# Four by-token tiles at once: 512 moving weight columns in place of 256

## What is computed

```python
def first_block(x, mem, ...):
    for layer in range(2):
        u = rms_norm(x, attn_norm_w[layer]) @ w_in[layer]       # 1024 -> 2560
        # layer 0: q, k, v, gate of 6 retention heads; layer 1: q, k, v of 6 differential heads
        # both: queries of 4 memory heads
        ...
        x = x + concat([o_main, o_mem]) @ w_out[layer]
        gu = rms_norm(x, ffn_norm_w[layer]) @ w_gate_up[layer]
        x = x + (silu(gate) * up) @ w_down[layer]

def second_block(x, ...):
    proj = rms_norm(x, norm_mix_w) @ w_in                       # 1024 -> 5648
    z, xbc, dt_raw, q, k, v, f_raw = split(proj)
    y_ssd = ssd_mixer(xbc, z, dt_raw, ...)                      # 16 heads, 2 groups, group RMS norm
    y_fox = fox_mixer(q, k, v, f_raw, ...)                      # 16 heads of 64: q and k normed per head,
                                                                # causal softmax with a forget bias
    x = x + concat([y_ssd, y_fox]) @ w_out
    x = x + conv_gated_mlp(rms_norm(x), ...)
```

## Time and profile before

| | before |
|---|---|
| device time, median of 3 runs | 1043.74 us (1040.57 to 1046.72) |
| device time of the profiled execution | 1040.6 us |
| its span, first to last instruction | 1038.8 us |
| granted TensorE clock, mean | 1.000 |
| PE busy | 1023.2 us, 98% of the span |
| DVE busy | 796.6 us, 77% |
| ACT busy | 635.1 us, 61% |
| HBM read | 172.39 MB, 167 GB/s over the span |

### The profile page before, as it was taken

One profiled execution on the slowest core, in us unless ns is written; L12 is line 12 of the kernel. 1 busy time (PEld: TensorE's weight loads), 2 busy tenths in 40 slices (PEclk: granted clock), 3 DMA queues, 4 the chain that ended last, 5 costly groups with the idle time before them and its releaser, 6 DMA issues.

```text
span 1038.8 us, 21815 instructions
## 1 busy us (share of the span) xinstructions
PE 1023.2 (98%) x7372; PEld 940.7 (91%) x7372; DVE 796.6 (77%) x1301; ACT 635.1 (61%) x1188; POOL 236.0 (23%) x204
## 2 busy tenths in 40 slices
PE   8999999999999999999999999999999999999998
PEld 7999988888889898888888899999898999999988
DVE  6875897877665988988777559978868579999843
ACT  7754776666555667766656456766666666656532
POOL 3200044544110000244543110000201024444300
DMA  8643476666655332666666664543343456555663
GB/s 299 183 134 100 124 223 193 186 195 180 200 187 184 122 103 71 211 192 186 191 188 188 195 196 144 178 153 117 121 123 123 141 163 184 183 183 182 189 197 98
DMA packets 52483, 174.36 MB, mean 168 GB/s; under 512 B 5952, under 2 KB 7232, under 8 KB 52288
## 3 DMA queue, kind: packets, MB, share of 16 engines
q1 hardware_dynamic: 52416, 173.46, 53.9%
HBM read 172.39 MB, written 1.05 MB: 167 GB/s over the span
## 4 chain that ended last, share of the span: by engine, by line
PE 56%; DVE 4%; ACT 2%; issue 1%; DMA 0%; DVEq 0%; SPq 0%; ACTq 0%
PE bank L769 9%; PE scores L765 8%; PE bank L765 7%; PE scores L769 6%; PE bank L767 6%; PE bank L768 6%; PE scores L767 3%; PE scores L768 2%; PE bank L795 2%; PE bank L796 2%; PE bank L797 2%; DVE ring_parts L1731 1%; ACT tmp L1519 1%; DMA ring_raw<-w_up 0%; PE bank L1151 0%
## 5 line engine op out<-in xcount | busy, mean ns | idle before, releaser
L1731 DVE TENSOR_TENSOR ring_parts<-ring_raw,ring_parts 128x1024 fp32r<-128x1024 f32 (+2 forms) x343 | 421.4, 1232 | 34.8 <-ACT ring_parts L1221 29.3
L1221 ACT ACTIVATE ring_parts<-ring_raw 128x1024 fp32r<-128x1024 f32 (+2 forms) x343 | 341.2, 997 | 64.2 <-PE scores L769 28.9
L769 PE MATMUL bank<-xw_parts,ring_parts 128*128 128x256 f32 x824 | 230.9, 280 | 0.0
L769 PEld LDWEIGHTS bank<-xw_parts,ring_parts 128*128 128x128 f32 x824 | 156.4, 190 | 0.0
L769 PE MATMUL scores<-xw_parts,ring_parts 128*128 128x256 f32 x528 | 147.3, 279 | 0.0
L767 PE MATMUL bank<-xw_parts,ring_parts 128*128 128x256 f32 x472 | 136.5, 289 | 0.3 <-DVE con L1876 0.2
L769 PE MATMUL bank<-act_parts,ring_parts 128*128 128x256 f32 x480 | 134.8, 281 | 0.0
L768 PE MATMUL bank<-xw_parts,ring_parts 128*128 128x256 f32 x472 | 133.4, 283 | 0.0
L765 PE MATMUL scores<-xw_parts,ring_parts 128*128 128x512 f32 x352 | 123.8, 395 | 0.7 <-DVE xw_parts L1737 0.7
L765 PE MATMUL bank<-xw_parts,ring_parts 128*128 128x512 f32 x352 | 123.4, 394 | 0.7 <-DVE xw_parts L1737 0.7
L795 PE MATMUL bank<-ring_parts,xw_parts 128*128 128x256 f32 x384 | 112.9, 294 | 0.2 <-DVE u L1919 0.2
(11 more groups left out here) (257 smaller groups left out, 2136.5 us busy)
## 6 DMA issues: line engine op xcount, KB each, us to landing
ring_raw<-w_up SPq DMA_DIRECT2D x132, 512.0 KB, 4.3
ring_raw<-w_in SPq DMA_DIRECT2D x85, 512.0 KB, 3.6
ring_raw<-w_down SPq DMA_DIRECT2D x48, 512.0 KB, 3.8
ring_raw<-w_down SPq DMA_DIRECT2D x24, 384.0 KB, 4.1
ring_raw<-w_oa SPq DMA_DIRECT2D x16, 256.0 KB, 2.6
ring_raw<-w_ob SPq DMA_DIRECT2D x16, 256.0 KB, 2.9
ring_raw<-w_oa SPq DMA_DIRECT2D x8, 512.0 KB, 3.6
ring_raw<-w_ob SPq DMA_DIRECT2D x8, 512.0 KB, 3.6
```

Of the source, the lines that this page charges most:

```text
L769: return mm(ps[:, 0:T], w_lo, high(parts, t), start=False, stop=stop)
L1221: A(ring_hi[:, slot * DM:slot * DM + width], ring_raw[:, slot * DM:slot * DM + width], ACT.Copy).then_inc(hi_done, 1)
L1731: V.tensor_tensor(ring_lo[:, a:b], ring_raw[:, a:b], ring_hi[:, a:b].bitcast(f32), SUB).then_inc(lo_done, 1)
```

## The change

What the diff does, part by part:

- Nine groups of four tiles each (`FOURS`: one in in0, two in in1, six in in2) take the place of eighteen pairs. A four holds the weights of 512 channels; each of its tiles has a quarter of the input rows (two blocks of 128) and 512 columns. `project_four` uses both banks at once, the first 128 tokens in one and the other 128 in the other: per tile six matmuls of 512 columns, then the steps that belong in the middle of the tile, then six more. A four is 48 matmuls of 512 columns where two pairs were 96 of 256; the count of TensorE rows falls from 4960 to 4528.
- A new semaphore, `first_tokens`, is raised in the last tile when the first bank is complete; DVE takes out each bank with one TENSOR_SCALAR of 128x512 (`evac_four`, L1870 of the new kernel): two instructions for two pairs as before.
- The tile orders change (`ORDER`): in in2 two query pairs stand together, then two key pairs, then four value tiles. Norms move with them: in layer 1 the ones of tiles 0 and 2 two slots later, in layer 2 the query and the key norm of a j are in neighbouring slots (24 and 25, 28 and 29, 36 and 37, 40 and 41) where they were two slots apart, and the values of the fox heads are read from slot 33 or 45 on.
- `after_like` puts `spread` and `norm_out` behind steps of the same kind where there are some. The per-head means have four buffers where there were two. `squares` of a norm whose norm n-2 is a per-head one waits for that one's head sum and not for its output.
- The host lays the weight columns out to match.

The diff, without the semaphore, the buffer's size and part of the host layout:

```diff
@@ -52,10 +52,11 @@
 SMALL = 44
-ORDER = {"in0": [18, 19, 0, 3, 6, 7, 1, 4, 8, 9, 2, 5, 10, 11, 12, 13, 14, 15, 16, 17],
+ORDER = {"in0": [18, 19, 0, 3, 1, 4, 6, 7, 8, 9, 2, 5, 10, 11, 12, 13, 14, 15, 16, 17],
          "in1": [18, 19, 0, 1, 6, 7, 2, 3, 8, 9, 12, 13, 4, 5, 10, 11, 14, 15, 16, 17],
          "in2": list(range(8, 20)) + [SMALL] + list(range(8))
-         + [t for j in range(4) for t in (20 + 2 * j, 21 + 2 * j, 28 + 2 * j, 29 + 2 * j, 36 + 2 * j, 37 + 2 * j)]}
+         + [t for j in range(0, 4, 2) for t in (20 + 2 * j, 21 + 2 * j, 28 + 2 * j, 29 + 2 * j, 22 + 2 * j, 23 + 2 * j,
+                                                30 + 2 * j, 31 + 2 * j, *range(36 + 2 * j, 40 + 2 * j))]}
@@ -116,6 +117,9 @@
+FOURS = {"in0": (6,), "in1": (0, 2), "in2": (20, 22, 24, 26, 36, 40)}
...
 HALVES = ("up0", "up1", "down0", "down1", "down2")
@@ -127,6 +131,10 @@
             self.wide = [c for c, t in enumerate(ORDER.get(name, [])) if t in BY_TOKEN[name] and t % 2 == 0]
+        self.fours = [ORDER[name].index(t) for t in FOURS.get(name, ())]
+        for c in self.fours:
+            self.wide.remove(c + 2)
+            self.wide.append(c + 1)
         self.name, self.n, self.blocks, self.ring0, self.out0 = name, n, blocks, ring0, out0
@@ -148,7 +156,11 @@
-        return c in self.wide or c - 1 in self.wide
+        return c in self.wide or c - 1 in self.wide or self.of_four(c) is not None
+    def of_four(self, c):
+        return next((c - a for a in self.fours if a <= c < a + 4), None)
@@ -157,7 +169,7 @@
-        return c % self.per == self.per - 1 and c not in self.wide
+        return c % self.per == self.per - 1 and c not in self.wide and self.of_four(c) is None
@@ -194,6 +206,12 @@
+    def after_like(layer, slot, step):
+        steps = plan[layer][slot]
+        n = next((i for i, other in enumerate(steps) if other[0] != step[0]), len(steps))
+        steps.insert(n, step)
     def norm(layer, slot, tile, soon=False):
@@ -201,11 +219,11 @@
         at(layer, slot + 1, "norm", tile)
-        plan[layer][slot + 2].insert(0, ("spread_soon" if soon else "spread", tile))
+        after_like(layer, slot + 2, ("spread_soon" if soon else "spread", tile))
         if soon:
         else:
-            plan[layer][slot + 3].insert(0, ("norm_out", tile))
+            after_like(layer, slot + 3, ("norm_out", tile))
@@ -257,7 +275,7 @@
-    for t, slot in ((18, 2), (0, 3), (6, 5), (2, 7), (8, 9), (4, 13), (10, 15)):
+    for t, slot in ((18, 2), (0, 5), (6, 5), (2, 9), (8, 9), (4, 13), (10, 15)):
         norm(1, slot, t)
@@ -317,20 +335,19 @@
     at(2, 18, "ssd_steps", 1)
-    for j in range(4):
-        a = 21 + 6 * j
-        norm(2, a + 2, 20 + 2 * j)
-        norm(2, a + 4, 28 + 2 * j)
-        if j:
-            for slot, ahead, t in ((a + 2, a + 1, 20 + 2 * j), (a + 4, a + 4, 28 + 2 * j)):
-                plan[2][slot].remove(("squares", t))
-                plan[2][ahead].insert(0, ("squares", t))
+    for j, end in enumerate((24, 28, 36, 40)):
+        for slot, t in ((end, 20 + 2 * j), (end + 1, 28 + 2 * j)):
+            norm(2, slot, t)
+            if j:
+                for at_, kind in ((slot, "squares"), (slot + 1, "norm")):
+                    plan[2][at_].remove((kind, t))
+                    plan[2][at_].insert(0, (kind, t))
         for n in range(2):
-            p, slot = 2 * j + n, a + 7 + 3 * n
+            p, slot = 2 * j + n, 28 + 6 * j + 3 * n
             at(2, slot, "fox_scores", p)
             at(2, slot + 2, "fox_weights", p)
-            at(2, slot + 3, "fox_values", p)
+            at(2, max(slot + 3, 33 if j < 2 else 45), "fox_values", p)
     for p in range(8):
...
@@ -590,10 +608,10 @@
-            return heads[:, 16 * (n % 2):16 * (n % 2) + 8]
+            return heads[:, 16 * (n % 4):16 * (n % 4) + 8]
         def head_roots(n):
-            return heads[:, 16 * (n % 2) + 8:16 * (n % 2) + 16]
+            return heads[:, 16 * (n % 4) + 8:16 * (n % 4) + 16]
@@ -633,6 +651,8 @@
                 last = order.index(t)
+                four = PH[f"in{layer}"].of_four(last)
+                last += 0 if four is None else 3 - four
                 eng.wait_ge(out_ready, PH[f"in{layer}"].out(0, last) + 1)
@@ -776,6 +796,9 @@
                 pe.wait_ge(lo_done, g + 1)
+                if ph.of_four(c) is not None:
+                    project_four(ph, c, parts, slot, halfway)
+                    return
                 if part == 0 and c - 1 not in ph.wide:
@@ -809,6 +832,28 @@
+            def project_four(ph, c, parts, slot, halfway):
+                part = ph.of_four(c)
+                for tt in range(2):
+                    n = ph.out(0, c - part) + tt
+                    if part == 0:
+                        pe.wait_ge(out_ready, ph.freed_out(n))
+                    if halfway and tt:
+                        halfway(c)
+                    for k in range(2):
+                        t = ph.inputs[2 * part + k]
+                        a = slot * DM + k * 2 * T
+                        o = bank[ph.bank_of[n]][:, :]
+                        w_hi, w_lo = ring_hi[:, a:a + 2 * T], ring_lo[:, a:a + 2 * T]
+                        x_hi, x_lo = (m(parts, t)[:, tt * P:(tt + 1) * P] for m in (high, low))
+                        mm(o, x_hi, w_hi, start=part == 0 and k == 0, stop=False)
+                        mm(o, x_hi, w_lo, start=False, stop=False)
+                        last = mm(o, x_lo, w_hi, start=False, stop=part == 3 and k == 1)
+                    if part == 3 and tt == 0:
+                        last.then_inc(first_tokens, 1)
+                last.then_inc(tile_done, 1)
             def project_first_two(ph, parts, ready):
@@ -1366,7 +1411,10 @@
                 arrived(act, layer, t + 1 if t < 64 and not (layer == 0 and t >= 37) else t)
-                if n >= 2:
+                before = [k for (kind, k), m in number.items() if kind == "head_stat" and number["norm", k] == n - 2]
+                if before:
+                    act.wait_ge(head_ms, number["head_stat", before[0]] + 1)
+                elif n >= 2:
                     act.wait_ge(np_out, n - 1)
@@ -1762,13 +1810,15 @@
                             split_lo(ph, j, d)
+                    if ph.wide and i == 0 and c == 3:
+                        root_by_token(q)
                     if ph.finishes(c):
                             refine(q)
-                        if ph.wide and i == 0 and c == 3:
-                            root_by_token(q)
                         dve.wait_ge(tile_done, ph.tile(i, c)[1] + 1)
                         evac(ph, i, c, bank[ph.bank(i, c)][:, 0:2 * T if ph.by_token(c) else T])
+                    if ph.of_four(c) == 3:
+                        evac_four(ph, c)
                     if before_split:
@@ -1800,6 +1850,24 @@
                                 rstd_tok[:, :].unsqueeze(2).to_broadcast([P, 2, T]), MUL).then_inc(out_ready, 1)
+            fours_done = [0]
+            def evac_four(ph, c):
+                fours_done[0] += 1
+                layer, t, t2 = int(ph.name[2:]), ORDER[ph.name][c - 3], ORDER[ph.name][c - 1]
+                for tt, (done, count_) in enumerate(((first_tokens, fours_done[0]), (tile_done, ph.tile(0, c)[1] + 1))):
+                    dve.wait_ge(done, count_)
+                    b = bank[ph.bank_of[ph.out(0, c - 3) + tt]]
+                    if heads_by_token(layer, t):
+                        q_and_k = u[:, t * T:(2 * t2 - t) * T].rearrange("p (n c) -> p n c", n=2)
+                        dst = q_and_k[:, :, tt * T:(tt + 1) * T]
+                        src = b[:, :].rearrange("p (n c) -> p n c", n=2)
+                    else:
+                        v, c0 = WIDE[layer, t]
+                        dst, src = v[:, tt * DM + c0:tt * DM + c0 + 2 * T], b[:, :]
+                    V.tensor_scalar(dst, src, rstd_tok[:, tt:tt + 1], None, MUL).then_inc(out_ready, 1)
...
@@ -2282,9 +2350,14 @@
-        return np.concatenate([wide_tiles(m[:, t * P:t * P + T]) if t in BY_TOKEN[name] else
-                               column_tiles(m[:, t * P:(t + 1) * P])
-                               for t in ORDER[name] if t not in BY_TOKEN[name] or t % 2 == 0])
+        out_, at_ = [], 0
+        while at_ < len(ORDER[name]):
+            t = ORDER[name][at_]
+            n = 4 if t in FOURS[name] else 2 if t in BY_TOKEN[name] else 1
+            cols = np.concatenate([m[:, f * P:(f + 1) * P] for f in ORDER[name][at_:at_ + n]], 1)
+            out_.append(wide_tiles(cols, n) if n > 1 else column_tiles(cols))
+            at_ += n
+        return np.concatenate(out_)
     w_in2 = a["w_in_2"][0]
     small[:, 0:16] = w_in2[:, 2560:2576]
```

7 lines of the change are left out of this document (4 added, 3 removed).

## The result

| | before | after |
|---|---|---|
| device time, median | 1042.15 us (1039.95 to 1046.72, 4 runs) | 1052.68 us (1048.33 to 1056.45, 4 runs) |
| ratio of the runs | | 1.0101, 95% interval 1.0066 to 1.0135 |
| span of the profiled execution | 1038.8 us | 1050.0 us |
| granted TensorE clock, mean | 1.000 | 0.993 |

The change made the kernel 1.0% slower, 10.5 us, where the forecast was 1044.0 with a range up to 1050.5. In six more runs it took 1053.4 us at a ratio of 1.0101 (1.0071 to 1.0130).

A forecast was written before the change was run, and what follows sets the result against it. TensorE, busy 98% of the span, was taken as the bound. New waits of 5.9 us less 5.6 us saved in matmuls gave 0.3 us slower, 1044.0 us in the median's measure; 8-in-10 range 1036 to 1050.5.

The forecast's parts named there:

- The two large waits: Layer 2, slots 29 and 41: squares wait for the group norm's output, delaying ScalarE's copies; TensorE waits 3.3 and 3.4 us.
- The last handover: End of layer 2's by-token tiles, slot 44: the reciprocal stands ahead of both evacuations; 1.0 us, bounds 0 and 2.9.
- The waits named as taken back: Old waits expected to vanish: 0.6 us before L1029 in layer 1, 2.1 after slot 29, 1.7 after slot 41.
- The other seven handovers: Bank handovers with only norms ahead of the evacuation, 0.7 us against 1.4 available: no cost.
- the first rival: Faster, the new waits are cheap: 6.4 us faster, 1037.3 us if both large waits cost nothing; chance 0.26.
- the second (all handovers wait): Slower: seven more handovers at 1.0 us each, 7.0 us more, 1051.0 us; chance 0.16.
- The new waits: Net new TensorE waits: 1.1 us in layer 1, 2.1 at slot 29, 2.7 at slot 41; sum 5.9 us.
- the clock: TensorE's granted clock, 1.000 before, so no stretch at the lower level; no cost was forecast for the changed kernel.
- one handover: Layer 2, slot 32 to 33, where the first values end: a wait of 0.7 us, bounds 0 and 2.
- a `spread`: Layer 2, middle of slot 28: a spread waits 0.2 us more.
- in1: Layer 1: norms sharing slots make the softmax 1.9 us later, 1.1 us more wait net, bounds 0 and 1.9.
- the matmuls: By-token matmuls of 512 columns at 0.227 us: a four saves 0.62 us, nine fours 5.6, ends 4.3 and 8.6.

The follow-up runs named there:

- the second trace: Trace from running the changed kernel again, nothing edited, beside the kernel before: 1053.4 us, ratio 1.0101.
- plan_without_fours: Changed kernel with FOURS empty: new tile order, norm places and semaphore waits kept, pairs of 256 columns everywhere; 1054.13 us, ratio 1.0107 to the kernel before.
- in1_pairs: Changed kernel with layer 1 undone: pairs there, norms of tiles 0 and 2 back at slots 3 and 7; 1050.84 us, ratio 1.0082 to the kernel before.

## Why the prediction was wrong

**Right.** The two large waits were named with their place, their releaser and nearly their size. Forecast 3.3 us before L1184 and 3.4 before the transposes; measured 3.56 and 3.58. The last handover, forecast 1.0, is 0.96 between starts. The waits named as taken back are gone. The other seven handovers cost next to nothing, and the first rival (the waits vanish) and the second (all handovers wait) did not come.

**The steps that failed.** Two terms of the sum carry the miss: the new waits, net 5.9 us in the prediction, and the clock, put at nothing. The size of a step below is an estimate from the lags of the traces. The new waits are the lag without falls of the clock plus what the fours save: 7.4 us in layer 2 (4.8 and 2.6) for 4.8 forecast, and 2.9 in layer 1 (2.0 and 0.9) for 1.1, so 10.3 us in place of 5.9. The clock took 2.1 us in place of none.

**Wrong in size: layer 2's waits, 2.6 us.** About 1.1 of it is in two terms: one handover (1.16 at slot 33 in the second trace for 0.7) and a `spread` (0.87 for 0.2), and 0.4 in the two large waits. The other 1.1 us are in no single wait above 0.3 us, and their cause stays open.

**Wrong in size: in1.** Forecast 1.1 us of waits less 1.2 gained, -0.1; measured +2.0. The wait at the first transposes was seen (1.9 late, measured 1.7 and 2.05 between starts). Those behind it at 380.9 and 389.5 (0.89 and 0.82) and the 0.5 more at L971 were not: I followed the late norms to the first softmax and took the next two for unchanged. The late places of the norms cost, two slots behind where pairs allow them: with them in1 takes 71.8 us without any four (plan_without_fours), and 69.1 with pairs and the early places (in1_pairs), while spacing the late norms out did not help.

**Put at nothing: that a stopped TensorE costs more than the time it stands.** The prediction read the granted clock of 1.000 and said that no stretch runs at the lower level, and left it there for a kernel with waits twice as long. The falls at those waits took 2.1 us of time in either trace of the changed kernel, about a quarter of the 7.9. With this term alone the forecast would have been 1046.1, well inside its range: the clock is a part of the miss and not the whole of it. The clock is no term of its own in the trace of before, but the question "what does an engine at 1.000 do when it first stands for 3 us" could have been asked.

**Wrong in size: the matmuls.** 0.226 to 0.227 us was taken from a stream of 512 by channel; by token it is 0.229 on the mean and 0.232 in the stretch shown. A four then saves 0.4 to 0.5 us and nine about 4, not 5.6. The lower end of that term in the prediction was 4.3. The Trainium skill's "TensorE: Matmul & The Clock Gate" (back-to-back issue), 1.1 us by its rule, is further from what was measured than the prediction, since 256 columns cost 0.120 here and not 0.109.

**Not shown to be the change's: the paces.** The prediction took the medians as they were, with the executions of before up to 6.6 us apart. About 2.5 of the 10.5 us are slow feed-forwards: 11 of the 20 in its ten executions by their times, 15 of 42 in the 21 of before beside it, too few to say that the change has a part in it.

The sum of the traces: 0.3 forecast, 2.6 and 1.1 for waits and matmuls in layer 2, 2.1 for in1 (0.3 of it matmuls), 2.1 clock, less 0.5 gained elsewhere (layer 0 and the output projection of layer 1): 7.7 of the 7.9 us, and with 2.5 of paces 10.2 of 10.5. Without the paces the kernel would stand near 1050, at the edge of the range: that the time lies outside it hangs on the paces too, and that it is 8 us slower where 0.3 was forecast is not.
